# Hybrid decoder step: order of key rotation, decode gate and factor stores in the first block

## The reference

```python
h = rmsnorm(x, norm_w)
z = h @ w_in          # GLA: q, k, v, gate, low-rank gate input; retention: q, k, v, gate
la = log_sigmoid(glr @ gla_w2 + gla_b) / 16                       # GLA log decay, per key column
q_b, k_b = rope(rq), rope(rk) * DK ** -0.5                        # retention: rotated by position
# GLA:       S_t = exp(la_t) * S_{t-1} + k_t^T v_t ;  o_t = q_t S_t
# retention: S_t = gamma_h  * S_{t-1} + k_t^T v_t ;  o_t = q_t S_t
o_a = rmsnorm_per_head(o_a) * gla_norm_w * silu(gg)
o_b = (groupnorm_per_head(o_b) * ret_norm_w + ret_norm_b) * silu(rg)
y = x + concat(o_a, o_b) @ w_out
```

## Time and profile before

| | |
|---|---|
| median of 3 runs | 1651.32 us (1649.62 to 1651.87) |
| profiled execution, its own time | 1652.58 us |
| its span | 1650.5 us |
| TensorE busy (PE) | 1636.9 us, 99% |
| VectorE (DVE) / ScalarE (ACT) / GpSimd (POOL) busy | 65% / 37% / 51% |
| mean granted clock of TensorE | 0.998 |
| weight half, issue to landing, median | 3.6 us |

### The profile page before, as it was taken

How to read it: one execution, slowest core, us unless ns; L and a number is a source line. 1 busy time by engine, 2 the same in 40 slices (tenths; PEclk the granted TensorE clock), 3 DMA queues, 4 the chain that set the end, 5 groups by cost and what they waited for, 6 DMA issues and landing times.

```text
span 1650.5 us, 26302 instructions
## 1 busy us (share of the span) xinstructions
PE 1636.9 (99%) x9792; PEld 1354.8 (82%) x9792; DVE 1070.1 (65%) x2378; ACT 617.8 (37%) x1152; POOL 834.2 (51%) x646
## 2 busy tenths in 40 slices
PE   9999999999999999999999999999999999999998
PEld 7788878888888887888878888788888888878887
DVE  5844776768764675457754367757887457784374
ACT  5414434234343343424452234342443324342342
POOL 4544545645445464445544445456554455554455
PEclk9999999999999999999999999999999999999999
DMA  8366656767455574466653656566864377553654
GB/s 290 99 112 168 195 208 153 205 192 233 144 105 153 164 198 129 127 161 160 184 149 96 163 142 190 164 189 183 189 194 135 108 169 163 173 173 99 146 154 141
DMA packets 389279, 268.18 MB, mean 162 GB/s; under 512 B 290720, under 2 KB 293152, under 8 KB 389152
## 3 DMA queue, kind: packets, MB, share of 16 engines
q1 hardware_dynamic: 315280, 131.99, 32.0%
q10 hardware_dynamic: 73872, 134.51, 26.2%
HBM read 219.34 MB, written 47.07 MB: 161 GB/s over the span
## 4 chain that ended last, share of the span: by engine, by line
PE 95%; DMA 2%; DVE 1%; SPq 1%; issue 0%; ACT 0%; ACTq 0%; POOLq 0%; POOL 0%; DVEq 0%
PE bank L781 82%; PE bank L1026 3%; PE bank L1032 2%; PE bank L986 2%; PE bank L1010 2%; DMA w_stage<-in_w_slots 1%; PE bank L875 1%; PE bank L747 1%; PE bank L807 1%; PE bank L864 0%; DMA xn<-in_x_t 0%; SPq L482 0%; DVE la L1691 0%; PE bank L909 0%; DMA k_n<-out_k_rows 0%
## 5 line engine op out<-in xcount | busy, mean ns | idle before, releaser
L280 POOL TENSOR_TENSOR w_lo<-w_stage,w_hi 128x512 fp32r<-128x512 f32 x344 | 479.1, 1412 | 472.6 <-ACT w_hi L273 472.2
L781 PE MATMUL bank<-h_hi,w_hi 128*128 128x512 f32 x1016 | 403.9, 398 | 2.5 <-ACT region L1174 1.5
L781 PE MATMUL bank<-h_lo,w_hi 128*128 128x512 f32 x1016 | 396.3, 390 | 0.0
L781 PE MATMUL bank<-h_hi,w_lo 128*128 128x512 f32 x1016 | 396.1, 390 | 0.0
L273 ACT ACTIVATE w_hi<-w_stage 128x512 fp32r<-128x512 f32 x344 | 199.7, 624 | 494.1 <-PE bank L781 437.6
L280 POOL TENSOR_TENSOR w_lo<-ss,w_hi 128x512 fp32r<-128x512 f32 x112 | 149.5, 1355 | 166.4 <-ACT w_hi L273 166.4
L781 PEld LDWEIGHTS bank<-h_hi,w_hi 128*128 128x128 f32 x1016 | 190.7, 188 | 52.0 <-issue 6.6
L781 PEld LDWEIGHTS bank<-h_hi,w_lo 128*128 128x128 f32 x1016 | 190.8, 188 | 40.5
L781 PEld LDWEIGHTS bank<-h_lo,w_hi 128*128 128x128 f32 x1016 | 190.9, 188 | 37.1
L781 PE MATMUL bank<-w_hi,m_hi 128*128 128x512 f32 (+1 forms) x520 | 201.6, 388 | 0.0
L781 PE MATMUL bank<-w_hi,h_hi 128*128 128x512 f32 x512 | 201.1, 393 | 0.0
(11 more groups left out here) (228 smaller groups left out, 2192.5 us busy)
## 6 DMA issues: line engine op xcount, KB each, us to landing
w_stage<-in_w_slots ACTq DMA_DIRECT2D x344, 256.0 KB, 3.6
ss<-in_w_slots ACTq DMA_DIRECT2D x112, 256.0 KB, 4.1
region<-in_x_prompt SPq DMA_DIRECT2D x32, 512.0 KB, 6.0
out_o_rows<-region SPq DMA_DIRECT2D x64, 256.0 KB, 3.1
v_b<-in_w_slots ACTq DMA_DIRECT2D x56, 256.0 KB, 3.0
region<-out_o_rows SPq DMA_DIRECT2D x192, 64.0 KB, 3.0
out_k_rows<-region SPq DMA_DIRECT2D x32, 256.0 KB, 3.3
k_n<-out_k_rows SPq DMA_DIRECT2D x256, 32.0 KB, 2.6
```

The lines of the kernel that those rows point to most:

```text
L280: pool.tensor_tensor(w_lo[:, r, c], stage(h), w_hi[:, r, c].bitcast(f32), ALU.subtract).then_inc(lo_done, 1)
L781: i = pe.matmul(dst, x, y, start=(s == 0 and kk == 0 and c == 0), stop=(s == 3 and kk == 1 and c == 2), skip_group_check=True)
```

## The change

Six edits, all in block 0 or ahead of it:

- VectorE rotates the two key tiles between the first and the second half of the gate, then does the second half, the decode gate, and the two query tiles. Before: both halves, key tiles, decode gate, query tiles.
- SP's queue stores the factor rows at w = 15, behind `turn_outputs(0)`.
- TensorE does slot 2 in two passes over the four banks, one for each K tile (k = 2, then k = 3), and waits for `h_lo` of a tile only ahead of its pass. The wait for `lo_done` of both halves stays ahead of the slot. `sample_sum` comes behind the first pass (12 products) instead of behind the first bank's 6.
- ScalarE issues the loads of halves 4 and 5 behind `h_hi` of tiles 2 and 3 instead of 0 and 1.
- The load of `ident` is issued behind the load of tiles 4 and 5.

```diff
--- before.py
+++ after.py
@@ -520,11 +520,11 @@
             load_first(0, 0, 1)
             load_nw(0)
             load_first(1, 1, 2)
-            sp.dma_start(ident[:, :], d["ident"]).then_inc(ident_in, 16)
             load_first(2, 2, 4)
             for dst, name in ((xs, "x_sample"), (gsum, "gsum")):
                 sp.dma_start(dst[:], d[name]).then_inc(first_in, 16)
             load_first(3, 4, 6)
+            sp.dma_start(ident[:, :], d["ident"]).then_inc(ident_in, 16)
             load_rows(0, (0, 1))
             load_par(0)
             load_rows(0, (2, 3))
@@ -557,7 +557,7 @@
                         turn_keys(n, w // 13)
                     if w == 10 and b == 0:
                         save_v(l, 0)
-                    if w == (13 if n == 0 else 9 if n < NBLK - 1 else 4) and n < LAST:
+                    if w == (15 if n == 0 else 9 if n < NBLK - 1 else 4) and n < LAST:
                         store_factors(n)
                     if w == 14:
                         turn_outputs(n, 0)
@@ -835,6 +835,15 @@
                             pe.wait_ge(mlo_first.sem, mlo_first.at(n, 2))
                         elif u == 6:
                             pe.wait_ge(mlo_sb.sem, mlo_sb.at(n, 2 * s))
+                        if n == 0 and w == 2:
+                            for k in (2, 3):
+                                pe.wait_ge(hlo_sb.sem, hlo_sb.at(0, k + 1))
+                                for q in range(4):
+                                    i = products(0, 1, q, (k - 2,))
+                                if k == 2:
+                                    sample_sum(0)
+                            i.then_inc(slot_used, 1)
+                            return
                         if n == 0 and u == 0:
                             pe.wait_ge(hlo_sb.sem, hlo_sb.at(0, 2 * s + 2))
                         for q in range(4):
@@ -842,8 +851,6 @@
                                 free_bank(u, q)
                             for cut in (slice(0, 256), slice(256, 512)) if n == LAST and u == 7 and q == 3 else (slice(0, 512),):
                                 i = products(u, s, q, cut=cut)
-                            if n == 0 and w == 2 and q == 0:
-                                sample_sum(0)
                             if n == 0 and w == 3 and q == 0:
                                 pe.wait_ge(ident_in, 16)
                                 sample_transposed(0)
@@ -1076,8 +1083,8 @@
             for k in range(4):
                 split_hi(act, k)
                 raw_hi(act, k)
-                if k < 2:
-                    load_half(act, 2 * AHEAD + k)
+                if k >= 2:
+                    load_half(act, 2 + k)
             raw_hi(act, 4)
             raw_hi(act, 5)
             for l in range(DEPTH):
@@ -1635,14 +1642,12 @@
                             wait_bank(vec, n, 4 + g, q)
                             vec.tensor_tensor(P[q][:, :], P[q][:, :], rb[:, :], ALU.mult).then_inc(first_g, 1)
 
-                    def rotate():
+                    def rotate(order, c):
 
                         vec.wait_ge(rope_in.sem, rope_in.at(n, 16))
                         if n == 0:
                             vec.wait_ge(first_rope, 1)
-                        vec.wait_ge(la_sb.sem, la_sb.at(n, 2))
-                        c = 0
-                        for i_ in (2, 3, 0, 1):
+                        for i_ in order:
                             buf = q_t[:, i_, :] if i_ < 2 else k_t[:, i_ - 2, :]
                             if i_ < 2:
                                 vec.wait_ge(q_raw.sem, q_raw.at(n, i_ + 1))
@@ -1650,8 +1655,6 @@
                                 vec.wait_ge(k_raw.sem, k_raw.at(n, i_ - 1))
                             if c > 0:
                                 vec.wait_ge(rope_st.sem, rope_st.at(n, c))
-                            if n == 0 and c == 8:
-                                sample_gate()
                             apart()
                             vec.stream_shuffle(r_tmp[:, :], buf, [(p + 16) % 32 for p in range(32)]).then_inc(rope_st.sem, 1)
                             vec.wait_ge(rope_st.sem, rope_st.at(n, c + 1))
@@ -1694,8 +1697,16 @@
                             for sgn in range(2):
                                 i = vec.tensor_scalar(nb[:, :, sgn, 2 * hf:2 * hf + 2], la[:, :, 256 * hf + MID:256 * hf + 256:TOK], (2.0 * sgn - 1.0) / TAU, None, ALU.mult)
                             i.then_inc(nb_sb.sem, 1)
-                        if w == 5:
-                            rotate()
+                        if n == 0 and w == 4:
+                            vec.wait_ge(la_sb.sem, la_sb.at(n, 1))
+                            rotate((2, 3), 0)
+                        if n == 0 and w == 5:
+                            sample_gate()
+                            vec.wait_ge(la_sb.sem, la_sb.at(n, 2))
+                            rotate((0, 1), 8)
+                        if n > 0 and w == 5:
+                            vec.wait_ge(la_sb.sem, la_sb.at(n, 2))
+                            rotate((2, 3, 0, 1), 0)
                         if w == 8:
 
                             vec.wait_ge(ex_sb.sem, ex_sb.at(n, 2))
```

## The result

| | before | with the change |
|---|---|---|
| median on the same chip | 1649.38 us (22 runs, 1648.22 to 1652.43) | 1652.74 us (22 runs, 1649.99 to 1655.77) |
| ratio, after to before | | 1.0018, interval 1.0012 to 1.0025 |
| profiled execution, its span | 1652.58, 1650.5 us | 1650.79, 1648.6 us |

The kernel became slower by 2.0 to 4.1 us (3.0 by the ratio). The forecast was 1.5 us faster (1649.8 us from the median of three runs shown then). Its range, 1647.3 to 1653.0, holds the new time; its side is wrong. One execution of the experiments, in row_stores, took 1935 us at a mean granted clock of 0.80 and is left out of its median and ratio.

A forecast was written before the change was run, and what follows sets the result against it. TensorE, busy 99% of the span, was taken as the bound, with 7.8 us of first-block waits and low clock aimed at. -4.8 + 3.1 + 1.6 + 0.1 - 1.5 = -1.5 us from median 1651.32: 1649.8 us, range 1647.3 to 1653.0.

The forecast's parts named there:

- The keys' new place, and VectorE's schedule behind it: Block 0, VectorE: rotation starts at 41.34 us, gate ends at 50.9, keys ready between 64 and 67, before TensorE's 67.38.
- The moved gate, +3.1 us: Block 0: gate 6.0 us later delays exponentials, split and w_lo; slot 8 starts at 57.2 instead of 54.12 us.
- The low clock behind it, +1.6: Block 0, slot 8: TensorE's idle time of 3.2 to 3.3 us brings the low clock; +1.6 us, ends 0 and 1.7.
- Rival B: Same exchange of waits ahead of slot 8, but the low clock doesn't come; -3.1 us, 1648.2 us; chance 0.26.
- The start, 0: Slots 2 and 3: the 1.0 us h_lo wait comes back as a w_lo wait; net 0, put at 0.1 us.
- The factor rows, -1.5: Stores moved behind the turned outputs: TensorE's 1.5 us wait for the value copy near 125 us goes; -1.5 us.
- Rival D: Moved factor rows meet weight loads without slack, making w_lo late; +4.1 us, 1655.4 us; chance 0.07.
- the prediction's own sign of D: A wait of TensorE between 130 and 160 us would show that the factor rows meet weight loads without slack.
- The 3.2 us wait goes, and the 1.6 us of low clock behind it: -4.8 us: Block 0, first state product: TensorE no longer waits for the turned keys, nor runs at low clock behind; -4.8 us.

The follow-up runs named there:

- row_stores: Kernel before, with block 0's factor rows stored as 128 floats side by side in one partition, at the same place; 1650.73 us, ratio 1.0002.
- keys_only: Kernel before with only VectorE's part of the change (key rotation between the scans, decode gate behind the keys); 1651.5 us, ratio 1.0018.
- start_only: Kernel before with only the start edits: slot 2 in two passes, loads 4 and 5 and the identity tile later; 1649.22 us, ratio 1.0004.
- keys_start_split: Kernel before with the change's VectorE and start parts, ScalarE splitting halves 14 and 15 ahead of its exponentials, factor rows at w = 13; 1647.23 us, ratio 0.9986.
- after_again: The whole change run once more, unedited, against the kernel before; 1653.57 us, ratio 1.0023.
- before_3: Kernel before, unchanged, third further execution with a trace; 1648.61 us, wait for the keys 1.9 us.
- before_2: Kernel before, unchanged, second further execution with a trace; 1649.94 us, wait for the keys 1.8 us.
- before_again: Kernel before, unchanged, first further execution with a trace; 1650.78 us, wait for the keys 3.2 us.

## Why the prediction was wrong

By its own steps:

- **The keys' new place, and VectorE's schedule behind it: right.** First half ends 41.14 (forecast 41.34), gate 50.54 (50.9), keys ready 67.3 (64 to 67), no wait for them. One reading was off without effect: before, all three multiplications and additions of the second key tile were stretched, not two of them.
- **The moved gate, +3.1 us: right but for some tenths**, with slot 8 at 56.72 against 57.2 and a wait of 3.3. Less the 0.5 us of the decode gate's wait, which is gone, that is +2.8.
- **The low clock behind it, +1.6: right for the traces and most runs**: 1.3 and 1.6 us in the two traces, 28 of 33 runs. Rival B, without it, is what keys_only's trace shows and what few runs of the change do.
- **The start, 0: right** to what a measurement can tell, with the 0.5 us ahead of slot 3 instead of 1 us.
- **The factor rows, -1.5: wrong.** The value copy wait of the earlier trace rows is in none of the traces of before taken later (of the others with the rows at that place, start_only has 0.3 us of it and keys_start_split 0.8). There was nothing to gain in a usual execution. Rival D's mechanism, held to be covered by ScalarE's slack, is there in a small form: ScalarE waits 8.5 us for a half, and TensorE 1.0 and 1.3 us behind it, in after_again (the prediction's own sign of D, a wait between 130 and 160 us); in the first trace of the change TensorE has none.
- **The term that made the sign: "The 3.2 us wait goes, and the 1.6 us of low clock behind it: -4.8 us".** This was mis-sized. Before, the wait is 1.7 to 1.9 us in five traces of nine, and the low clock is behind it in 3 of 9 traces and at most a quarter of the runs. So the term is -1.7 to -1.9 for the wait in an execution with the shorter one and -2.5 in the mean of the traces, and on average -0.4 for the clock (a quarter of 1.6): -2.3 to -2.9 instead of -4.8.

With those sizes the same sum reads, for an execution of before with the shorter wait: -1.9 (keys) -0.4 (clock) +2.8 +1.4 (1.6 in 28 of 33 runs) and 0 for the start and the factor rows: +1.9 us; with the mean wait of the traces, +1.3. With the waits behind 150 us, where they come, it is up to 2.3 more. Measured are 2.0 to 4.1.

The traces of block 0 bear this out. The first product of its output projection starts here (TensorE, in before_3, then in the first trace of the change and in after_again):

```profile
179.17 0.50 PE L781 MATMUL bank<-w_hi,m_hi 128*128 128x512 f32 x1
```

```profile
181.65 0.50 PE L781 MATMUL bank<-w_hi,m_hi 128*128 128x512 f32 x1
```

```profile
184.35 0.48 PE L781 MATMUL bank<-w_hi,m_hi 128*128 128x512 f32 x1
```

In before_2 it is 179.79, in before_again 181.13, and in the trace shown ahead of the prediction 184.03, as late as in after_again. So the change is 2 us later there than the shorter wait of before, and 5 us with the waits behind 150 us. From there to the end all 17 traces take 1466.5 to 1468.5 us, whichever version it is.

The error behind it is one of reference. The sum was made against the profiled execution, 1652.58 us, and then moved under the median of three runs, as if the waits of the one were those of the others. That execution is above all of the 22 runs of before listed beside the change. Its low clock alone (1.6), its long scaling (1.0) and its value copy (1.5) were 4.1 us that an execution of before with the shorter wait doesn't have, and all three were entered as gains. The low clock is in three of the nine traces, the long scaling in four, the 1.5 us for the value copy in that one alone. The prediction had even written down that the profile was 1.3 us above the median, and left it at that.

What stays open: the interval of keys_only (1.5 to 4.5 us) is met by its sum of -1.9 -0.5 -0.4 +3.3 +1.2 = +1.7 only at its lower end, with the clock counted at 8 runs in 11, and missed by some tenths with the mean wait of 2.5. Up to some 3 us of it have no row. Whether the late single floats cost 1 us on average or none is not told apart either.

## What to carry to other kernels

A wait that stands in one profile is worth what it lasts in a usual execution: before entering a stall as a gain, ask whether this execution was a slow one, and which of its waits hang on a race between two engines, or bring a low clock in some executions only; a second and a third trace of the same kernel show it. When work of one engine is moved, look at what it stood beside: moving GpSimd's w_lo off VectorE's rotation gained as much as any version, and needed no new order on VectorE. And where an in-order engine waits for late work, first put what doesn't depend on it ahead of the wait.

## What the runs showed of the hardware

- VectorE's scaling of the keys (128x1024) takes 1.23 us when it starts 0.14 to 0.35 us ahead of GpSimd's w_lo (five traces), and 1.73 to 2.27 us when it starts 0.08 to 0.62 us behind (four traces). A wait of TensorE changed from 3.2 to 1.8 us with that, and with it the chance of a low clock.
- An idle time of 3.2 to 3.3 us of TensorE is followed by the 1.2 GHz level in some executions and not in others, of one kernel too (5 of 7 traces in all); behind 1.4 to 1.9 us it was in none of 6. The Trainium skill (TensorE: Matmul & The Clock Gate, What's actually happening) calls the count of slow matmuls at the start of a kernel "run-variable"; the traces show it behind a wait in mid-kernel too: the 32 state products behind 3.2 us take 3.48 us in the first trace of before and 1.97 in before_again. Matmuls whose results nobody needs, put into the wait, kept the clock at 2.4 GHz in all 11 runs and took the ratio from 1.0018 and 1.0023 to 1.0006.
- Four stores of 128 single floats slow the packets of other transfers behind them, those of weights on ScalarE's queue too, for 8 to 18 us. Packets that took over 1 us, up to 4.8 and 7.6, stood from 107.4 to 115.5 us in keys_start_split and from 126.5 to 144.5 in after_again; with rows of 512 B there are single ones of 1.0 to 1.5 us and no such stretch.
